# Moving the slots of TensorE's weights by 128 bytes against its other operands

## The reference

```python
for i in range(2):
    h = rmsnorm(x, norm_mix[i])
    m = stick_breaking_attention(h, ...) if i == 0 else retention(h, ...)   # 16 heads of 64; 4 heads of 256/512
    x = x + m
    a = rmsnorm(x, norm_ffn[i]) @ ffn_w_in[i]                # 1024 -> 2 x 2816
    gate, up = a[..., :2816], a[..., 2816:]
    x = x + (silu(causal_conv3(gate)) * up) @ ffn_w_out[i]   # 2816 -> 1024
    x = x + sigmoid(rmsnorm(x, norm_pl[i]) @ pl_w_gate[i]) * (p[i] @ pl_w_proj[i])
return rmsnorm(x, norm_final)
```

## The kernel before, in words

| tensor | address before | modulo 512 | modulo 1024 |
|---|---|---|---|
| `xh`, `xl` | 16768, 33152 | 384 | 384 |
| `raw` | 49536 | 384 | 384 |
| `wh`, `wl` | 61824, 84352 | 384 | 384 |
| `oh`, `ol` | 186752, 203136 | 384 | 384 |
| `yh`, `yl` | 134528, 179584 | 384 | 384 |
| `pinh`, `pinl` | 125824, 129920 | 384 | 896 |
| `vy`, `sums_h`, `sums_l` | 142208, 183168, 199552 | 384 | 896 |

## Time and profile before

### The profile page before, as it was taken

The page is one execution under the profiler, slowest core; times in us unless marked ns, Lnnn a source line. Parts: engine busy times, 40 slices in busy tenths (PEclk is TensorE's granted clock), DMA queues, the critical chain, the costliest instruction groups (busy, mean ns, idle before and its releaser), DMA issues.

```text
span 1497.6 us, 19989 instructions
## 1 busy us (share of the span) xinstructions
PE 1483.6 (99%) x6808; PEld 1235.1 (82%) x6808; DVE 847.6 (57%) x1294; ACT 675.7 (45%) x1019; POOL 797.0 (53%) x980
## 2 busy tenths in 40 slices
PE   9999999999999999999999999999999999999997
PEld 6888888888888888888888888888888888888886
DVE  7999997455555411169874655646755555511145
ACT  6887886433323322247573543635623332322243
POOL 5343344666666755457345253551666666755452
PEclk9999999999999999999999999999999999999999
DMA  5121111332322322243133322321232222332221
GB/s 179 57 71 55 43 56 60 110 98 98 98 98 98 127 98 97 86 165 103 56 141 99 111 90 89 133 99 43 87 110 95 97 89 97 119 113 96 94 83 58
DMA packets 42838, 142.14 MB, mean 95 GB/s; under 512 B 4256, under 2 KB 10528, under 8 KB 42784
## 3 DMA queue, kind: packets, MB, share of 16 engines
q1 hardware_dynamic: 41248, 138.82, 27.4%
q10 hardware_dynamic: 1536, 2.61, 0.5%
HBM read 139.32 MB, written 2.10 MB: 94 GB/s over the span
## 4 chain that ended last, share of the span: by engine, by line
PE 96%; DVE 2%; ACT 1%; DMA 1%; issue 0%; POOL 0%; SPq 0%; POOLq 0%; DVEq 0%; ACTq 0%
PE bank L605 27%; PE bank L608 26%; PE bank L609 26%; PE bank L883 3%; PE bank L888 3%; PE bank L887 3%; PE bank L683 2%; PE bank L663 1%; PE bank L664 1%; PE bank L694 1%; PE bank L693 1%; DMA x<-in_xT 1%; PE bank L1036 0%; DVE sumsq L1125 0%; PE bank L666 0%
## 5 line engine op out<-in xcount | busy, mean ns | idle before, releaser
L551 POOL TENSOR_TENSOR wl<-raw,wh 128x256 fp32r<-128x256 f32 x752 | 617.4, 853 | 471.2 <-ACT wh L1711 471.2
L605 PE MATMUL bank<-xh,wh 128*128 128x512 f32 (+1 forms) x1160 | 451.3, 389 | 0.7 <-DVE xl L1131 0.4
L609 PE MATMUL bank<-xh,wl 128*128 128x512 f32 (+1 forms) x1160 | 449.9, 388 | 0.0
L1711 ACT ACTIVATE wh<-raw 128x1024 fp32r<-128x1024 f32 (+1 forms) x212 | 235.0, 1108 | 476.0 <-PE bank L605 384.2
L608 PE MATMUL bank<-xl,wh 128*128 128x512 f32 (+1 forms) x1160 | 449.7, 388 | 0.0
L605 PEld LDWEIGHTS bank<-xh,wh 128*128 128x128 f32 x1160 | 217.9, 188 | 46.6 <-DVE xl L1131 1.7
L609 PEld LDWEIGHTS bank<-xh,wl 128*128 128x128 f32 x1160 | 217.8, 188 | 45.2
L608 PEld LDWEIGHTS bank<-xl,wh 128*128 128x128 f32 x1160 | 217.9, 188 | 43.3
L567 POOL TENSOR_TENSOR wl<-raw,wh 128x256 fp32r<-128x256 f32 x160 | 127.2, 827 | 190.6 <-ACT wh L1711 190.6
L1151 DVE TENSOR_TENSOR x<-x,bank 128x512 f32<-128x512 f32 x56 | 38.5, 687 | 250.7 <-PE bank L609 250.7
L605 PE MATMUL bank<-yh,wh 128*128 128x512 f32 x352 | 136.9, 389 | 0.0
(11 more groups left out here) (224 smaller groups left out, 2325.5 us busy)
## 6 DMA issues: line engine op xcount, KB each, us to landing
raw<-in_w SPq DMA_DIRECT2D x180, 512.0 KB, 3.2
raw<-in_w SPq DMA_DIRECT2D x32, 704.0 KB, 4.1
rc<-in_w SPq DMA_DIRECT2D x16, 512.0 KB, 4.2
w_end<-in_w SPq DMA_DIRECT2D x8, 512.0 KB, 4.1
rb<-in_w SPq DMA_DIRECT2D x8, 512.0 KB, 6.0
x<-in_xT SPq DMA_DIRECT2D x4, 512.0 KB, 7.0
pin<-in_pT ACTq DMA_DIRECT2D x2, 512.0 KB, 3.4
rotary<-in_consts ACTq DMA_DIRECT2D x1, 512.0 KB, 3.5
```

The source lines that it names most:

```text
L551: last = nc.gpsimd.tensor_tensor(wl[:, slot, cols], part[:, cols], wh[:, slot, cols].bitcast(F32), ALU.subtract)
L605: first = mm(out, ah_, bh_, start=start, stop=False, skip_group_check=True)
L609: return mm(out, al_, bh_, start=False, stop=stop, skip_group_check=True)
L1711: nc.scalar.activation(out, in_, ACT.Copy, bias=0.0, scale=scale).then_inc(done, 1)
```

## The change

Two tensors that only take up room: a new one of 32 words (128 bytes of each partition) ahead of `wh`, and `operands_at` grows from 8 to 104 words (by 384 bytes).

```diff
         raw = sb("raw", [RAW_COLS])
+        sb("weights_at", [32])
         with ExitStack() as ph:
             wh, wl = sb("wh", [RING, FH * P], F32R, ph), sb("wl", [RING, FH * P], F32R, ph)
         w_end = sb("w_end", [2, RING, FH * P])
         par = sb("par", [G_COLS])
         eps, turn = sb("eps", [1]), sb("turn", [1])
 
-        sb("operands_at", [8])
+        sb("operands_at", [104])
```

## The result

| | before | after |
|---|---|---|
| time, median | 1499.28 us (1499.12 to 1499.57, 4 runs) | 1533.25 us (1531.62 to 1534.82, 4 runs) |
| ratio | | 1.0226, 95% interval 1.0214 to 1.0238 |
| profiled execution: time, span | 1499.36, 1497.6 us | 1534.82, 1533.0 us |

The forecast was 1499.4 us, the range 1476 to 1521. The time lies 12 us above the range.

What follows compares the result with a forecast made beforehand. The prediction took the time as the number of TensorE matmuls times the distance between their starts. The profiled 1499.36 us (span 1497.6 plus 1.76) plus 0 from all parts gave 1499.4 us, range 1476 to 1521.

Steps and rivals of the forecast that it cites:

- What bounds the kernel: Whole kernel: TensorE's matmuls fill 99% of the span, so only the distance between their starts can move the time.
- parts 3 and 4: ScalarE and GpSimd writing the slots, and loads into slot ends: both priced 0, the loads ±1 us at most.
- Part 1: Matmuls with one operand in a slot: 5826 of 512 columns, so 1 ns of distance is worth 5.8 us.
- Part 2: Distance between those matmuls' starts: 226.6 ns, of which 13.0 ns could depend on addresses; change priced at zero.
- the 3.4 ns of the earlier trace: Attention stream at 230.0 ns, 3.4 ns slower with the same operands; worth 19.8 us, up to 1519.2 us.
- The slower rival: Slot matmuls: the shift puts the two SBUF reads' meeting mid-load; 19.8 us more, 1519 us; chance 0.28.
- The faster rival: Slot matmuls: reads meeting at each matmul's start are what costs; 37.9 us less, 1461 us; chance 0.24.
- the remainder: In each matmul, 13.0 ns (about 31 cycles) beyond its columns' time, said to be all an address can act on.
- What would show it: First MLP: 89 distances again take 20.17 us; 19.6 if the faster case holds, 20.5 if the slower.

Runs made afterwards that it cites:

- second map: Kernel without the model, zeros stored: 49 stretches of 49 matmuls at varied operand offsets, operands alternating between two tensors; 226.67 ns at difference 0, 232.3 at 128.
- x apart: Against the kernel before, slots and all tensors behind them moved 128 bytes, leaving x, xh, xl and raw 128 off: 1520.83 us, ratio 1.0144.

## Why the prediction was wrong

*What bounds the kernel* was right: the whole difference is the distance between starts, waits did not grow, and the writers of the slots, the transfers and the clock gave nothing (parts 3 and 4).

*Part 1, the number of matmuls,* holds with a correction. 5826 x 6.67 ns is 38.9 us; 35.4 came. The MLP's second products pay in full (1056 x 6.67 = 7.04 us, and 7.04 measured). The attention pays less, 3.12 us where 768 matmuls would pay 5.12. Its short matmuls cut the projections' stream into runs of 12 to 24, and after a cut the starts need some distances to settle. The 230.0 ns of the earlier trace rows are just that: eight of the first nine starts after a cut. From where those rows end, 156.30 us, the next 15 distances take 3.40 us, 226.7 ns:

```profile
159.70 0.39 PE L609 MATMUL bank<-xh,wl 128*128 128x512 f32 x1
```

Over the whole attention up to 220 us neighbouring matmuls with a slot stand 228.4 ns apart before and 232.5 after. The retention pays less too, 8.60 us where its 1434 matmuls with a slot would pay 9.6. The tail of 256 columns pays nothing.

*Part 2 is the step that failed.* I priced the change of the distance at 0 ns; it was 6.67 ns in the steady stream, and that makes the 35.4 us. I took zero because over one load the two read addresses sweep a whole period, so that "each relative position modulo 512 is passed about once per load" whatever the start. The runs show that the start does matter: in the second map 0 and 256 bytes give 226.67 ns and every other difference more, even 4 bytes. The sweep argument counts clashes as if each were independent of the last. The records show instead patterns that repeat over several matmuls (in the changed kernel's first product distances of about 229 and 238 ns take turns), so that what one start does carries on to the next. That is a description; by what mechanism it does so is not shown. A second fault lies in the bounds: the 3.4 ns of the earlier trace rows was no bound, only a congruent stream settling after an interruption, and the range followed it. The true figure was twice that.

*The slower rival* had the sign and the carrier (a relation of the two reads, 0.28 of chance) but not the picture or the price: a meeting in the middle of the load would be cheap at 32 bytes and as dear at 256 as at other distances, and 32 costs 36.6 us, 256 nothing. *The faster rival* is refuted by the map: nothing is below 226.67, and half the remainder was added, not taken away.

*What would show it:* the 20 us stretch told it at once: 89 distances of 233.4 ns are 20.8 us, beyond the 20.5 us that I gave the slower rival. The tail was to show the same difference per matmul; it showed none. The matmuls with no operand in a slot were to keep their distances; they did not quite (the groups of `vy` with `shl`, 120 matmuls, went from 226.7 to 228.2 ns on average). They stand between matmuls with a slot, whose rhythm may carry over; that was not tried by itself. A stage that is congruent throughout did keep it (`yh` with x apart: 119.73 against 119.68 us).

The Trainium skill ("SBUF — State Buffer", section "Who interferes with whom") gives TensorE two independent read ports and lets it wait on nobody. No run here shows another engine slowing TensorE's steady stream, which agrees. But the place of one of TensorE's own operands against the other changed its stream by 6.67 ns of 226.67 in float32, so the measurement decides against reading the rule as "addresses don't matter to TensorE".

What stays open: what inside is shared. With blocks of 128 columns the excess was seen only in float32 and only off a difference of 0 modulo 256, and in full only at 512 columns. Why one stretch at 16 bytes escaped it, what chooses among the rhythms, and whether the stream, the own block or the next load is held up is not shown. Nor is what the 13.3 ns at congruent addresses are (the same at 256, 320, 384, 416 and 512 columns, but 16.0 at 448 and 16.7 at 480).

## What to carry to other kernels

In a float32 (fp32r) kernel that TensorE bounds, put every stationary block of 128 columns and every moving operand of 512 columns at the same address modulo 256 bytes, and check it again whenever a tensor is added, since 32 bytes cost 2.4% here. Read the distance between starts in a steady stretch (226.67 or 233.33 ns), not the busy share, which was 99% in both. If two stages with the same loop stand at different distances, or runs of one kernel scatter by 0.4% on one core, look at the operands' addresses first.

## What the hardware showed that I had not expected

- The distance of a float32 stream of 512 columns and blocks of 128 depends on the two operands' addresses modulo 256: 226.67 ns when equal, up to 234.4 when not; in bfloat16 215.9 at 0 and at 128. One stretch off by 16 bytes ran at 226.7 all the same.
- Away from equal addresses the same code has more than one rhythm: 228.2 and 236.7 ns in one kind of stretch, 228.9 and 233.3 in two layers of one execution.
- A smaller stationary block is not cheaper: 231.5 ns with 32 columns, 226.67 with 128.
- After an interruption a congruent stream can need up to nine distances to settle, at 224 to 236 ns each, before it keeps 226.67.
